# Norms whose token scales are applied behind the products, and a recurrence without logarithms, on one Trainium2 core

## What is computed

```python
def rms_norm(x, g):
    y = x * lax.rsqrt(jnp.mean(x * x, axis=-1, keepdims=True) + EPS)
    return y * g

def rg_lru(x, w_a, b_a, w_i, b_i, lam, reverse):           # width 512, forward and backward
    r = sigmoid(block_diag(x, w_a) + b_a)
    i = sigmoid(block_diag(x, w_i) + b_i)
    log_a = -8.0 * r * softplus(-lam)
    a = jnp.exp(log_a)
    mult = jnp.sqrt(-jnp.expm1(2.0 * log_a))
    b = mult * (i * x)
    return scan of h = a * h + b over the tokens

# layer 1
h = rms_norm(x, attn_norm);  proj = h @ w_in
lru_out = (rg_lru(forward) + rg_lru(backward)) * gelu(yg)
mla_out = latent attention of 8 heads (low-rank queries, keys and values)
x = x + concat(rms_norm(lru_out), rms_norm(mla_out)) @ w_out
x = x + memory_attention(rms_norm(x, mem_attn_norm), rms_norm(mem, mem_norm))
x = x + convolved gated feed-forward of rms_norm(x, ffn_norm)
# layer 2
x = x + dilated_and_differential_attention(rms_norm(x, attn_norm_2))
x = x + (silu(u @ w_gate) * (u @ w_up)) @ w_down,  u = rms_norm(x, ffn_norm_2)
# layer 3
x = x + hgrn(rms_norm(x, hgrn_norm_2))
x = x + moe(rms_norm(x, moe_norm_2))                       # 8 experts, 2 per token
```

## Time and profile before

| what | value |
|---|---|
| median of 3 runs | 2012.64 us (2012.32 to 2013.17) |
| the profiled execution | 2013.82 us, of which its span 2011.9 |
| PE busy | 1893.1 us, 94% |
| PE weight load | 1593.1 us, 79% |
| DVE busy | 1545.1 us, 77% |
| ACT busy | 1257.6 us, 63% |
| POOL busy | 26.8 us, 1% |
| PE's granted clock, mean of the span | 0.967 of 2.4 GHz |

### The profile page before, as it was taken

The page is one execution under the profiler, slowest core; times in us unless marked ns, Lnnn a source line. Parts: engine busy times, 40 slices in busy tenths (PEclk is TensorE's granted clock), DMA queues, the critical chain, the costliest instruction groups (busy, mean ns, idle before and its releaser), DMA issues.

```text
span 2011.9 us, 27381 instructions
## 1 busy us (share of the span) xinstructions
PE 1893.1 (94%) x10190; PEld 1593.1 (79%) x10190; DVE 1545.1 (77%) x1548; ACT 1257.6 (63%) x1285; POOL 26.8 (1%) x13
## 2 busy tenths in 40 slices
PE   7866899999889999999699999999999999999997
PEld 7665699877669987977588888888888888888886
DVE  7864488657655555664798898988989889898897
ACT  7954565445644434543477777777777777777775
POOL 0300000000000000000200000000000000000000
PEclk9987899999979999999899999999999999999998
DMA  8322154543225554432299899998999989999894
GB/s 353 134 92 84 63 184 176 190 163 126 84 86 187 180 182 162 147 126 105 95 352 368 326 364 342 351 369 322 364 343 351 364 323 365 343 355 366 320 366 186
DMA packets 68041, 490.83 MB, mean 244 GB/s; under 512 B 7681, under 2 KB 7937, under 8 KB 8577
## 3 DMA queue, kind: packets, MB, share of 16 engines
q1 hardware_dynamic: 67680, 488.52, 64.9%
q0 software_dynamic: 288, 1.31, 0.2%
HBM read 488.75 MB, written 1.05 MB: 243 GB/s over the span
## 4 chain that ended last, share of the span: by engine, by line
PE 86%; DVE 6%; ACT 5%; issue 2%; DMA 0%; SPq 0%; ACTq 0%; DVEq 0%
PE ps L393 26%; PE ps L395 20%; PE ps L402 20%; PE ps L404 5%; PE ps L397 5%; PE ps L413 2%; DVE wl L1863 1%; PE ps L1162 1%; ACT wh L1238 1%; PE ps L1074 1%; PE ps L893 1%; PE ps L930 1%; PE ps L666 1%; PE ps L667 1%; PE ps L671 0%
## 5 line engine op out<-in xcount | busy, mean ns | idle before, releaser
L2659 DVE TENSOR_TENSOR wl<-raw,wh 128x2048 fp32r<-128x2048 f32 x336 | 763.0, 2288 | 81.5 <-ACT wh L1779 81.3
L1779 ACT ACTIVATE wh<-raw 128x2048 fp32r<-128x2048 f32 x336 | 642.4, 1916 | 196.2 <-PE ps L402 195.9
L393 PE MATMUL ps<-wh,work_r 128*128 128x512 f32 x1544 | 614.9, 398 | 4.0 <-DVE work_r L2664 2.4
L395 PE MATMUL ps<-wh,work_r 128*128 128x512 f32 x1544 | 613.0, 397 | 0.0
L402 PE MATMUL ps<-wl,work_r 128*128 128x512 f32 x1544 | 449.4, 396 | 0.0
L1863 DVE TENSOR_TENSOR wl<-raw,wh 128x2048 fp32r<-128x2048 f32 x125 | 290.4, 2325 | 141.8 <-ACT wh L1238 141.4
L393 PEld LDWEIGHTS ps<-wh,work_r 128*128 128x128 f32 x1544 | 290.4, 188 | 71.7 <-issue 6.9
L402 PEld LDWEIGHTS ps<-wl,work_r 128*128 128x128 f32 x1544 | 290.3, 188 | 70.4
L395 PEld LDWEIGHTS ps<-wh,work_r 128*128 128x128 f32 x1544 | 290.6, 188 | 68.9
L1238 ACT ACTIVATE wh<-raw 128x2048 fp32r<-128x2048 f32 x125 | 238.7, 1912 | 97.2 <-PE ps L402 92.8
L393 PE MATMUL ps<-hTh,wh 128*128 128x256 f32 x896 | 224.4, 287 | 1.2 <-DVE hTl L1895 0.9
(11 more groups left out here) (387 smaller groups left out, 1712.5 us busy)
## 6 DMA issues: line engine op xcount, KB each, us to landing
raw<-in_units SPq DMA_DIRECT2D x461, 1024.0 KB, 6.6
x<-in_x SPq DMA_DIRECT2D x1, 1024.0 KB, 5.1
work<-in_lru_w SPq DMA_DIRECT2D x1, 1024.0 KB, 15.5
xn<-in_mem SPq DMA_DIRECT2D x1, 1024.0 KB, 16.6
out<-x SPq DMA_DIRECT2D x2, 512.0 KB, 3.5
consts<-in_consts POOLq DMA_DIRECT2D x1, 768.0 KB, 7.2
work<-in_moe_gain POOLq DMA_DIRECT2D x1, 512.0 KB, 3.8
consts<-in_consts SPq DMA_DIRECT2D x1, 488.0 KB, 5.7
```

Of the source, the lines that this page charges most:

```text
L393: nc.tensor.matmul(out, sh, mh, start=(first and j == 0), stop=False)
L395: nc.tensor.matmul(out, sl, mh, start=False, stop=False)
L1779: A(wh[:, n % SPLIT, :], raw[:, n % RAW, :], ACT.Copy).then_inc(sem("hi_made"), 1)
L2659: V.tensor_tensor(wl[:, n % SPLIT, :], raw[:, n % RAW, :], wh[:, n % SPLIT, :].bitcast(F32), ALU.subtract).then_inc(sem("lo_made"), 1)
```

## The change

**Norms scaled later.** A norm scales each token's row by one number. That number can be applied behind the product as well, since it is the same for all features of a token. For the three norms in `SCALED_LATER`, PE transposes x itself as soon as its residual halves are there, and the high and low halves are made from it; squares, mean, root and reciprocal are made behind them. The scale is applied where results leave PSUM: for `mem_attn_norm` and `attn_norm_2` the tokens lie on the partitions there, and ACT's copies take it as their scale (the copy of the values in two pieces). For `ffn_norm_2` the tokens lie along a row: DVE makes a diagonal matrix of the scales, PE multiplies it with ones (after the first gate-and-up tile), ACT copies the row out, and DVE multiplies each gate-and-up tile with it, before the sigmoid.

**The recurrence.** With t the tanh of `log_a`, `1 - a*a = -(a*a + 1)*t`, so DVE forms a*a and (a*a + 1)*t, and ACT takes the root of its negative. The logarithms, the exponentials that follow them and the two `lru_rooted` products go. GpSimd's four products move to DVE.

**Order.** PE sums the recurrence's squares ahead of the product for keys and values. The weight units 12 to 16, `hi_to(14)`, and the squares of the memory's keys take other places; the root of those keys stands behind the attention, ahead of the attention's own. The transposes of `attn_norm_2` go to the first banks, those of `ffn_norm_2` to the second four.

```diff
@@ PE
         def norm(name):
             i = NORM_OF[name]
+            if name in SCALED_LATER:
+                for t in range(TT):
+                    for c in range(KD):
+                        if c % 4 == 0:
+                            pe.wait_ge(*reached("x_ready", NORM_NEEDS[name] - 3 + 2 * t + c // 4))
+                        ins = nc.tensor.transpose(ps[:, NORM_BANK[name] + c // 2, (c % 2) * S + t * P:(c % 2) * S + (t + 1) * P],
+                                                  x[:, t, c * P:(c + 1) * P], ident)
+                        if t == TT - 1 and c % 2 == 1:
+                            counted(ins, "norm_transposed")
+                fresh[:] = [i, 0]
+                return
...
+        pe.wait_ge(*reached("mla_q_copied", 1))
+        pe.wait_ge(*reached("lru_sq", 1))
+        counted(accumulate(ps[:, 0, 0:S], [(ones, th[0][:, c, :]) for c in range(LC)]), "lru_ssq")
+
         w = unit(UNITS_AT["w_ukv"])
...
+                if f == 0 and stage == "ffn2":
+                    pe.wait_ge(*reached("scale_diag", 1))
+                    counted(accumulate(ps[:, 4, 0:S], [(ones, scale_diag.rearrange("p t c -> p (t c)"))]), "scale_ps")
@@ ACT
         def norm(name, ahead):
-            norm_stats(name)
-            norm_high(name, ahead)
+            if name in SCALED_LATER:
+                A(warm, ones[:, 0:1], ACT.Sqrt)
+                norm_high(name, 0)
+                norm_stats(name)
+                hi_to(ahead)
+            else:
+                norm_stats(name)
+                norm_high(name, ahead)
...
         hi_to(10)
-        act.wait_ge(*reached("lru_tanh", 8))
-        for d in range(2):
-            A(root[d], th[d][:], ACT.Ln, scale=-1.0, bias=ones[:, 0:1]).then_inc(sem("lru_ln"), 1)
-        for d in range(2):
-            act.wait_ge(*reached("lru_ln", d + 1))
-            A(root[d], root[d], ACT.Exp, scale=-0.5).then_inc(sem("lru_root"), 1)
...
-        for d in range(2):
-            act.wait_ge(*reached("lru_ln", 2))
-            A(th[d][:], th[d][:], ACT.Sqrt, scale=-2.0).then_inc(sem("lru_mult"), 1)
         mem_copied(0)
         mem_copied(1)
+        for d in range(2):
+            act.wait_ge(*reached("lru_span", d + 1))
+            A(th[d][:], th[d][:], ACT.Sqrt, scale=-1.0).then_inc(sem("lru_mult"), 1)
...
-        sqrt_of(heads_st[1][:, 40:48], heads_st[0][:, 40:48], "mem_k_ms", "mem_k_std")
-        act.wait_ge(*reached("lru_outT", 1))
-        attention("mla", {5: UNITS_AT["w_out"] + 4, 8: UNITS_AT["w_out"] + 5})
+        act.wait_ge(*reached("lru_outT", 1))
+        attention("mla", {5: UNITS_AT["w_out"] + 4, 7: UNITS_AT["w_out"] + 5})
+        sqrt_of(heads_st[1][:, 40:48], heads_st[0][:, 40:48], "mem_k_ms", "mem_k_std")
...
-        for f in range(FT + 1):
+        scales(1)
+        for f in range(FT + 2):
+            hi_to(UNITS_AT["ffn_gate_up"] + f + 4)
             if f < FT:
-                act.wait_ge(*reached("ffn2_gu", f + 1))
-                A(sg[f % 4], ps[:, f % 4, 0:S], ACT.Sigmoid).then_inc(sem("ffn2_gated_sigmoid"), 1)
-                hi_to(UNITS_AT["ffn_gate_up"] + f + 4)
+                act.wait_ge(*reached("ffn2_gated_read", f + 1))
+                A(sg[f % 4], gu2[f % 4][:, 0, :], ACT.Sigmoid).then_inc(sem("ffn2_gated_sigmoid"), 1)
@@ POOL
-        G_.tensor_tensor(z, yg[:], yg[:], ALU.mult).then_inc(sem("gelu_sq"), 1)
-        for d in range(2):
-            pool.wait_ge(*reached("lru_sigmoid", 4 * (d + 1)))
-            G_.tensor_tensor(ri[d][:], ri[d][:], xc[d][:], ALU.mult).then_inc(sem("lru_product"), 1)
-        pool.wait_ge(*reached("gelu_sig", 1))
-        G_.tensor_tensor(yg[:], yg[:], z, ALU.mult).then_inc(sem("gelu"), 1)
         pool.wait_ge(*reached("mla_kv", 4))
         pool.dma_start(consts[:, CONST["dist"]:], consts_d[:, CONST["dist"]:]).then_inc(sem("dist_loaded"), 16)
@@ DVE
+            if name in SCALED_LATER:
+                V.reciprocal(rstd[:, 2 * i:2 * i + 2], std[:, 2 * i:2 * i + 2]).then_inc(sem("norm_xn"), TT)
+                if name in BY_ROW:
+                    dve.wait_ge(*reached("norm_xn", TT * (i + 1)))
+                    for t in range(TT):
+                        ins = V.tensor_scalar(scale_diag[:, t, :], ident, rstd[:, 2 * i + t:2 * i + t + 1], None, ALU.mult)
+                    ins.then_inc(sem("scale_diag"), 1)
+                return
...
         for d in range(2):
-            dve.wait_ge(*reached("lru_product", d + 1))
-            dve.wait_ge(*reached("lru_root", d + 1))
-            V.tensor_tensor(ri[d][:], ri[d][:], root[d], ALU.mult).then_inc(sem("lru_rooted"), 1)
+            dve.wait_ge(*reached("lru_a", 4 * (d + 1)))
+            dve.wait_ge(*reached("lru_tanh", 4 * (d + 1)))
+            step(V.tensor_tensor(a2[d], ra[d][:], ra[d][:], ALU.mult))
+            V.scalar_tensor_tensor(out=th[d][:], in0=a2[d], scalar=1.0, in1=th[d][:], op0=ALU.add,
+                                   op1=ALU.mult).then_inc(sem("lru_span"), 1)
...
-        lo_to(13)
+        lo_to(12)
...
                                    op0=ALU.mult, op1=ALU.mult).then_inc(sem("lru_scaled"), 1)
+        lo_to(13)
         head_ms(1, msk, 1.0)
...
-        attention("mla", {0: lambda: lo_to(15), 2: mem_keys, 6: lambda: lo_to(16), 9: lambda: lo_to(17)})
+        attention("mla", {1: lambda: lo_to(14), 3: lambda: lo_to(15), 4: mem_key_squares, 6: lambda: lo_to(16)})
...
+            if f < FT:
+                dve.wait_ge(*reached("ffn2_gu", f + 1))
+                V.tensor_tensor(gu2[f % 4], ps[:, f % 4, :].rearrange("p (i s) -> p i s", i=2), both,
+                                ALU.mult).then_inc(sem("ffn2_gated_read"), 1)
```

112 lines of the change are left out of this document (69 added, 43 removed).

## The result

The changed kernel took 1991.93 us in the median (1991.41 to 1994.64, four runs), against 2012.48 (2011.94 to 2013.17) for the kernel before: a ratio of 0.990 with a 95% interval of 0.9883 to 0.9918, 20.5 us faster. The forecast was 1999.1 with a range of 1995 to 2004. The profiled execution took 1991.48, 22.3 less than the 2013.82 of before.

What follows compares the result with a forecast made beforehand. PE was taken to bound the kernel. Norms 13.9, recurrence 0.3, latent attention 0.95, less 1.6 for GpSimd's load, made 13.55 off the profiled 2013.82: 2000.3, and 1999.1 us for the median; range 1995 to 2004.

Steps and rivals of the forecast that it cites:

- what bounds it: Whole kernel: 86% of the span ends on PE, so only PE's waits before the experts can be won.
- the three norms: Memory attention, dilated attention, second feed-forward: PE transposes unscaled x earlier; 5.2 + 5.2 + 3.7 - 0.2 = 13.9 us.
- PE's clock at the norms: At mem_attn_norm and attn_norm_2: shorter idle gap, lower clock not expected again; 5.2 us each instead of 4.04.
- the recurrence up to the reciprocal: First mixer: first weighted product near 76.9, output at 90.1, reciprocal at 97.0 at full clock or 99.3 at half.
- the sum: Whole kernel: 13.9 + 0.3 + 0.95 - 1.6 = 13.55 us gained.
- the first mixer: Recurrence and latent attention: 0.3 us from the recurrence and 0.95 from the root's earlier start after the attention.
- After the latent attention: PE's 4.75 us wait behind the attention: memory keys' root takes ACT's table load first, so 0.95 us earlier.
- the GpSimd term: Ahead of the MoE products: library load, taken as 7 us, partly covered by idle time and slack, delays routing 1.6.
- Gains kept in full: Rival: library load covered (1.6 us back) and recurrence's sum of squares at full clock (1.9 back): 1995.6 us; chance 0.12.

Runs made afterwards that it cites:

- norms_only: The kernel before with only the three norms scaled later; recurrence, GpSimd's products and latent attention's order as before: 1996.97 us (ratio 0.9926).
- warm3: The changed kernel plus thirty unused transposes in PE's idle gap at each of three norms of the old form: 1991.09 us (ratio 0.9900).
- pool_products: The changed kernel with the recurrence's four products back on GpSimd: 2000.61 us (ratio 0.9938).
- after_delay2: The changed kernel plus two DVE fills of 128x512 ahead of the mean of the third layer's first norm: 1997.68 us.
- warm_moe: The changed kernel plus thirty unused transposes at three old-form norms, and 46 and 30 more in two routing waits: 1994.54 us (ratio 0.9906).
- keys_first: The changed kernel with the memory's key squares and weight unit 14 put back ahead of the latent attention: 2001.08 us (ratio 0.9944).
- early_lib: The changed kernel plus one unused 128x1 GpSimd product, meant to load its library ahead of the routing: 1992.48 us (ratio 0.9901).
- norm_ffn2: The kernel before with only the second feed-forward's norm scaled later, by the row of scales: 2007.97 us (ratio 0.9983).

## Why the prediction was right, and where it was wrong

**Right: what bounds it, and the three norms.** The low halves start 1.96 to 1.97 us behind the last addition at all three (forecast 2.04), so each chain is 4.1 shorter; the second group of products 5.03 earlier (5.2); the second feed-forward 3.68 (3.7), with the row of scales hidden as counted. The term was 13.9. norms_only measured 15.9, but with what changed behind the norms in it. The stages themselves say more: over all eighteen profiles, those with a norm in the new form against those with it in the old, the means of the three stages differ by 4.9, 5.6 and 3.5, together 13.9. That the memory stage gained 6.56 in the profiled pair was luck: it took 55.5 to 59.5 in six profiles with the old norm and 51.0 to 54.6 in twelve with the new one.

**Right: PE's clock at the norms.** I added 1.2 us to each of two norms, partly because the transposes no longer follow an idle gap. At `attn_norm_2` 0.9 of it came (5.03 beside 4.12 for the first low half). Timeline of PE in the kernel before:

```profile
436.75 0.78 PE L666 MATMUL ps<-wh,hTh 128*128 128x512 f32 x1
437.33 0.63 PE L667 MATMUL ps<-wh,hTl 128*128 128x512 f32 x1
437.75 0.60 PE L666 MATMUL ps<-wh,hTh 128*128 128x512 f32 x1
438.18 0.40 PE L667 MATMUL ps<-wh,hTl 128*128 128x512 f32 x1
```

The first three start 0.42 to 0.58 us apart, at a granted clock of 0.50, and the later ones 0.23. From the first product to the second group it was 3.51 us (436.75 to 440.26) and is 2.83 (423.89 to 426.72): 0.7 of the 0.9 is products at the lower clock. The last 0.2 lies between the first low half and the first product, where PE was still at its slow transposes before. At the third layer's norm, in the old form, warm3 found nothing to win from the clock, because there a weight subtraction of DVE stands ahead of the first low half.

**Right: the recurrence up to the reciprocal.** 77.31, 90.50 and 99.21 for 76.9, 90.1 and 99.3. The rule that I cited, the Trainium skill, SBUF — State Buffer, Who interferes with whom, holds in pool_products as it did in the trace of before: with GpSimd at work again, the two subtractions took 6.69 and the small operation 2.01.

**Wrong: the sum.** These are the steps that failed. The sum was 13.9 for the norms, 1.25 for the first mixer and -1.6 for GpSimd's load, and nothing for any other code: 13.55. The runs show 13.9, 3.4, 0, and 2.8 more in the third layer; routing and experts took 0.5 more in the mean of the changed kernel's three profiles than in that of the two of before. Together that is 19.6, and the three measured gains are 19.6, 20.5 and 20.7. The largest error is the term that the sum didn't have; the next is the first mixer's, 2.15 too small; then the load's 1.6.

**Wrong: no term for the stages behind.** The sum held only the parts that the change touches and took all other code to cost what it cost before, and the range had no room for more. The third layer brought 4.77 in the profiled pair. Its time goes by how often the lower clock comes at the tiny score products, and the kernel before had three such stretches in both of its profiles: at 844, 895 and 902 us its granted clock was low while PE was busy. I read the windows at the norms alone. In three profiles of the changed kernel there were none, two and one: 168.9 in the mean, 2.8 less than 171.75. Whether the changed kernel has fewer of them for a reason of its own or by the way its stages fall in time stays open. Six kernels close to it (after_delay2, warm3, warm_moe, keys_first, pool_products, early_lib) had three, none, three, three, one and none.

**Wrong: "After the latent attention" as the only place where the order wins.** The step counted 0.95 there, and PE's idle time before those transposes fell by 1.07: it is 3.68 in all eleven profiles with the root in its new place and 4.66 to 4.76 in the seven with the old order. It left out that the key squares and a subtraction no longer stand ahead of the attention's first maximum. From the transposes of queries and keys to the first head's it is 13.1 in the nine profiles with the whole of the new recurrence and order, and 14.15 to 15.02 (mean 14.65) in the seven with the old ones: 1.55, of which keys_first gives back 1.2. Six of those seven also have a stretch at the lower clock in these heads, at 120 to 127 us, and none of the nine has; norm_ffn2, the one without it, has the 14.15. The transposes of queries and keys came 0.6 earlier in the mean of the nine than in that of the seven (110.5 and 111.2), where I took 0.3. That is 3.2 of the 3.4 by which the first mixer as a whole is shorter (171.6 in the mean of the nine, 175.0 in that of the seven).

**Wrong: the GpSimd term.** 1.6 us were taken off for a library load that no row of mine showed, from a transfer of another kind. It is 0: the rows of 940.91 are those of before, and early_lib is no faster. The 6 us that the Trainium skill, GPSIMD Engine Reference, section 2.1, gives for a first call do not show here: from the load's instructions at 937.5 to the first product it is 3.4 us, the wait for `moe_gain` included, and as long without the load. Before, the load stood at 0.8 us of the 48.77 in which I could not place it.

No scenario of the prediction is what happened. "Gains kept in full", to which I gave 0.12, asked for a covered load, which came, and for a sum of squares at full clock, which did not (3.65 us). Its 1995.6 was still 3.7 us too long.

## What to carry to other kernels

A per-token scale commutes with the product: take it out of the chain between an addition and the next transposes, apply it as the results are copied out, and count on the whole chain less the low halves, 4 to 5 us here each time. Before you forecast a kernel that PE bounds, list its stretches at the lower clock over the whole span, those in code that is not touched as well: each one where PE sets the pace was about 1.5 us here that another version, or the next execution, may or may not have, and it belongs in the range. When two versions differ by less than about 5 us, compare medians and stages of several profiles; a stage whose code is the same tells how much of the difference is luck. When a norm starts earlier in one version, measure from the norm's own start: warm3's low halves came at 774.93 and not 775.26, and the whole stage had started 0.33 earlier.
